# Two expert-layer edits of a hybrid diffusion block: where four query units stand, and how one-hot rows are summed

## The chip, the cores and the metric

The kernel runs on one core of one Trainium2 chip. The metric is the device time of one execution in microseconds. The engines are TensorE (PE; its weight loads are shown as PEld), VectorE (DVE), ScalarE (ACT), GpSimd (POOL) and SyncE (SP, which only starts transfers). ScalarE and GpSimd start transfers too.

## The reference, cut to what matters

Two layers over 256 latent tokens of 1024 values, with 256 context tokens beside them (the context's second layer is needed for its keys and values only). Each layer has a mixer of four branches, and then a product-key expert layer. Only the latter is touched:

```python
def chunk(xc):                                   # 128 tokens
    q = (xc @ wq).reshape(128, 8, 2, 128)
    s1 = einsum('thd,hnd->thn', q[:, :, 0], k1)  # 8 heads, 128 keys
    s2 = einsum('thd,hnd->thn', q[:, :, 1], k2)
    v1, i1 = top_k(s1, 16); v2, i2 = top_k(s2, 16)
    cand = v1[..., :, None] + v2[..., None, :]
    cidx = i1[..., :, None] * 128 + i2[..., None, :]
    top_s, pos = top_k(cand.reshape(128, 8, -1), 16)
    eidx = take_along_axis(cidx.reshape(128, 8, -1), pos, -1)
    g = softmax(top_s, -1)
    h = gelu(einsum('thkd,td->thk', eu[eidx], xc))
    return einsum('thk,thkd->td', g * h, ev[eidx])
```

So each token has 8 x 16 = 128 experts. An expert is one row of 2048 float32 values (1024 of `eu`, 1024 of `ev`).

## The kernel before

**Tiles and passes.** The 256 tokens of a stream are two tiles of 128. Three passes through the expert layer are made: the latent tokens of the first layer (LAT0, `BL0`), the context tokens of the first layer (CTX0, `BC0`), the latent tokens of the second (LAT1, `BL1`). An expert pass goes token by token: GpSimd gathers the 128 rows of a token, one a partition, into one of eight slots of `ring` (L726, 1 MB). TensorE broadcasts the token's own row from `xr` into PSUM (L1215, two halves). VectorE multiplies and sums (L2063, two halves). After four tokens, a group, ScalarE takes the Gelu (L1547), VectorE the weights (L2073), and TensorE sums the `ev` halves (`weigh`, L1197), which sets their four slots free. The rows in `xr` come from DRAM (`xrows`) by small transfers that ScalarE's queue starts (`x_rows`, L1536): those of the first two groups stand in front of a pass's first token, the others behind each Gelu.

**The order of work.** Each engine runs its own program, written out at build time from one `SCRIPT`. A generator `yield`s after each step, and `Weave.run` (L134) then lets `SHARE` tokens of the expert pass follow, the same number on each engine. A step `TILE_READY` makes another 128 tokens available and lets GpSimd ask for up to seven tokens' rows at once (`ask_ahead`, L729). In `ask` (L710), a slot of the first eight is given free only when the query units that read it are multiplied, since `ring` holds the query weights before: token n needs second-tile unit 2n+1 (L723).

**The part in front of an expert pass.** For the two latent passes this is `apart`, written once for each engine (PE L939, ACT L1363, DVE L1955). With no `yield` within it, PE makes 16 query units of the first tile (`unit(0, u)`, eight 128x128 products each, L960) and 16 of the second (`unit(1, u)`). Behind each four of them is one score product (`scores`, L972). ScalarE copies each unit (L1375) and each score group (L1382). VectorE meanwhile searches the first tile's scores (`top16`), joins candidates, decodes positions, and picks the expert numbers (`picked`, L1929). It then hands `ts` to ScalarE for an exponential (`tsub`; `chosen`, L1421), weighs it (`weighted`, L1948) and reports `sel`. PE transposes the expert numbers and weights (L995, L996), ScalarE copies them to `eT` and `gT` (L1425, L1426), and the pass begins. The second tile's searches (`late`, eight steps with 2.4 tokens each, then `sel`) go between the tokens of the first.

**The queues.** Before the change, ScalarE's copies of all 16 second-tile units and of `scores(1, 3)` stand in front of `chosen`. On PE, all of these units, `scores(1, 3)` and the eight turns of `uT` (L993) stand in front of the two transposes. SyncE may load the next tile of `W` when `scores(1, 3)` is done (the `sc_ps` count, L551).

**Picking.** `picked` compares a position with 16 numbers (L1934), multiplies the one-hot rows by the indices (L1936) and sums each row of 16 (L1937). All three are chained by a semaphore, in bf16, with a float32 result. In the first tile of the latent passes it runs over four heads (1024 values a partition), four times. In their second tile and in both context tiles it runs over eight heads (2048), twice each.

Of the kernel before, what the change touches and what calls it, by code (L numbers as in the profile page):

```python
# [7 lines left out]
ALU = mybir.AluOpType  # L8
ACT = mybir.ActivationFunctionType
AX = mybir.AxisListType.X  # L10

D = 1024
P = 128
# [105 lines left out]
TILE_READY = "tile ready"  # L119

LATE = 8

# [90 lines left out]
def build(nc, x, ctx, ccols, cols_c, w_ada, w_rows, w_in, w_gate, w_out, w_q, w_key, b_in, nat_bias, gqa_sink, peer_uv0, peer_uv1,  # L213
          ident_c, wave_c, band_c, iota_c, strip_c, out):
    es = ExitStack()
    with es:
# [36 lines left out]
        ident = sb("ident", [P, P])  # L253
# [65 lines left out]
        isel_a = part(mix, 2 * TILE - 2 * HEADS * TOPK, [2, HEADS * TOPK])  # L319
# [8 lines left out]
        ts = part(small, 1024, [HEADS, TOPK])  # L328
# [13 lines left out]
        def bank(i, a=0, b=512):  # L342
            return PS[:, i * 512 + a:i * 512 + b]
# [398 lines left out]
        def _(pe):  # L742
            T = nc.tensor
# [195 lines left out]
            def apart(b, a):  # L939
# [36 lines left out]
                for u in range(16):  # L976
# [3 lines left out]
                    if u == 6:  # L980
                        pe.wait_ge(a["xn"], a.at("xn", TT))
                        pe.wait_ge(a["xread"], a.at("xread", 1))
                        turned(0, lambda k: scratch[:, 1, k * P:(k + 1) * P]).then_inc(a["xnT"], 1)
                for u in range(16):
                    unit(1, u)
                    if u == 0:
                        scores(0, 3)
                    if u and u % 4 == 0:
                        scores(1, u // 4 - 1)
                scores(1, 3)  # L990
                pe.wait_ge(a["u_ready"], a.at("u_ready", TT))
                pe.wait_ge(a["wo_s"], a.at("wo_s", KD + 32))
                turned(2, lambda k: uT[:, k, P:TOK]).then_inc(a["urow"], 1)  # L993
                pe.wait_ge(a["sel"], a.at("sel", 1))
                T.transpose(bank(6, 0, P), isel_a[:, 0, :], ident[:, :])  # L995
                T.transpose(bank(6, P, 2 * P), ts[:, :, :].rearrange("p h k -> p (h k)"), ident[:, :]).then_inc(a["selT"], 1)  # L996
                yield TILE_READY
                for q in range(LATE):
# [237 lines left out]
        def _(act):  # L1236
# [126 lines left out]
            def apart(b, a):  # L1363
# [30 lines left out]
                for u in range(16):  # L1394
# [5 lines left out]
                    if u == 12:  # L1400
                        rows_out(0)
                for u in range(16):
                    unit(1, u)
                    if u == 0:
                        scores(0, 3)
                    if u and u % 4 == 0:
                        scores(1, u // 4 - 1)
                scores(1, 3)
                chosen(b, a, 0, 6)
                yield TILE_READY  # L1410
                for q in range(LATE):
                    yield "late"
# [150 lines left out]
        def _(dve):  # L1563
# [365 lines left out]
            def picked(tt, h0, nh, e, hot, index):  # L1929
# [6 lines left out]
                ch.link(V.tensor_tensor(one4, one4, iv[:, :, e, :].unsqueeze(2).to_broadcast([P, nh, TOPK, TOPK]), ALU.mult))  # L1936
                ch.link(V.reduce_sum(index[:, e, m0:m1], one, AX))  # L1937

# [267 lines left out]
```

## Time and profile before

| | |
|---|---|
| median of three runs | 3242.15 us (3241.61, 3242.15, 3261.65) |
| the profiled execution | 3264.46 us, span 3262.7 us |
| TensorE busy | 2525.2 us, 77% |
| VectorE busy | 1908.4 us, 58% |
| GpSimd busy | 971.6 us, 30% |
| ScalarE busy | 490.4 us, 15% |
| read from memory | 1011.32 MB |
| mean granted TensorE clock | 0.767 of full |

Busy shares are means over very different stretches: the fronts (units on TensorE), the three selections, and the token loop in which a gather, VectorE and TensorE take turns. Times of a row are counted from the start of the span. A number in square brackets behind a row of a timeline is the time that the engine stood idle before it, and what ended it. TensorE's float32 products are shown as two records each, so 64 records of L960 are four units.

### The profile page before, as it was taken

The numbers are of one execution on the slowest core, as the hardware profiler recorded it, in microseconds if no ns is written. First come the engines' busy times: TensorE is split into PE (matmuls) and PEld (weight loads), VectorE is DVE, ScalarE is ACT, GpSimd is POOL, SyncE is SP. The second block draws the span as 40 slices with busy tenths as digits, with TensorE's granted clock in tenths as the row PEclk, the third lists the DMA queues.
The fourth block names the chain that finished last, engine by engine and source line by source line (L and its number), as shares of the span: only waits on it lengthen the run. The fifth ranks groups of instructions, "written<-read, shape, count | busy, mean of one in ns | idle before, by whom it ended". The sixth has DMA issues, their size and how long they took to land.

```text
span 3262.7 us, 34104 instructions
## 1 busy us (share of the span) xinstructions
PE 2525.2 (77%) x11632; PEld 1304.6 (40%) x11632; DVE 1908.4 (58%) x6024; ACT 490.4 (15%) x1063; POOL 971.6 (30%) x968
## 2 busy tenths in 40 slices
PE   6879986597899978837989987676898557766655
PEld 5768882053355544403544441111788101111111
DVE  3658987746544456785444445555438765555554
ACT  2141120013322210001012220000412000000000
POOL 0730002258222222221672223332000333333332
PEclk7989996587799988756988876656999556566566
DMA  7607737898899988766989999999240889999997
GB/s 307 239 30 291 299 143 286 316 376 299 316 392 370 360 333 354 289 260 264 373 329 411 411 373 389 401 395 367 89 137 11 336 326 402 399 404 372 400 399 299
DMA packets 147887, 1023.54 MB, mean 314 GB/s; under 512 B 18817, under 2 KB 19329, under 8 KB 28033
## 3 DMA queue, kind: packets, MB, share of 16 engines
q0 software_dynamic: 110592, 805.36, 62.1%
q1 hardware_dynamic: 30496, 202.36, 16.0%
q10 hardware_dynamic: 6624, 13.64, 1.1%
q8 instruction: 92, 1.51, 0.2%
q14 instruction: 83, 0.67, 0.1%
HBM read 1011.32 MB, written 9.96 MB: 313 GB/s over the span
## 4 chain that ended last, share of the span: by engine, by line
PE 47%; DMA 20%; DVE 16%; POOL 7%; issue 6%; ACT 3%; ACTq 0%; DVEq 0%; POOLq 0%; SPq 0%
DMA ring<-in_peer_uv,eT 19%; PE PS L1197 12%; PE PS L887 7%; DVE ring L2063 6%; PE PS L1215 6%; POOL ring L726 5%; PE PS L822 3%; PE PS L960 3%; PE PS L908 3%; PE PS L1090 2%; PE PS L892 2%; PE PS L1041 2%; PE PS L1132 1%; DVE ring L1615 1%; POOL mix L609 1%
## 5 line engine op out<-in xcount | busy, mean ns | idle before, releaser
L2063 DVE CUSTOM_DVE_ANT_0 ring<-ring,PS 128x512 f32<-128x512 f32 x1536 | 994.6, 685 | 833.0 <-PE PS L1215 479.7
L726 POOL DMA_INDIRECT ring<-in_peer_uv,eT x768 | 728.5, 949 | 2154.8 <-PE PS L1197 1355.1
L1215 PE MATMUL PS<-xr,onesb 3*128 3x512 bf16 x1536 | 643.6, 485 | 439.7 <-DVE hcol L2063 375.5
L1197 PE MATMUL PS<-ring,zcol 128*32 128x512 f32 x3072 | 592.6, 912 | 104.6 <-DVE zcol L2073 102.3
L1215 PEld LDWEIGHTS PS<-xr,onesb 3*128 3x128 bf16 x1536 | 113.8, 96 | 1053.7 <-DVE hcol L2063 543.0
L1197 PEld LDWEIGHTS PS<-ring,zcol 128*32 128x32 f32 x3072 | 104.1, 143 | 411.9 <-issue 235.9
L887 PE MATMUL PS<-uT,W 128*128 128x256 f32 x1024 | 252.9, 396 | 7.5 <-issue 7.5
L1547 ACT ACTIVATE ge<-hdot 128x4 f32<-128x4 f32 x192 | 39.5, 206 | 1418.3 <-DVE hdot L2068 1379.1
L887 PEld LDWEIGHTS PS<-uT,W 128*128 128x128 f32 x1024 | 195.2, 196 | 67.7 <-issue 41.5
L1615 DVE CUSTOM_DVE_ANT_0 ring<-ring 128x1024 f32<-128x1024 f32 x160 | 205.7, 1326 | 8.2 <-DMA ring<-in_w_rows 3.3
L822 PE MATMUL PS<-uT,W 128*128 128x256 f32 x672 | 170.0, 408 | 18.5 <-ACT uT L1279 18.5
L822 PEld LDWEIGHTS PS<-uT,W 128*128 128x128 f32 x672 | 132.8, 203 | 59.9 <-issue 21.3
L908 PE MATMUL PS<-uT,W 128*128 128x256 f32 x512 | 143.5, 428 | 0.0
L2063 DVE DVE_READ_ACCUMULATOR2_ANT hcol<- 128x1 f32 x1536 | 126.8, 83 | 0.0
L908 PEld LDWEIGHTS PS<-uT,W 128*128 128x128 f32 x512 | 101.2, 208 | 52.7 <-issue 39.6
L960 PE MATMUL PS<-uT,ring 128*128 128x128 f32 x1024 | 120.4, 279 | 0.0
L960 PEld LDWEIGHTS PS<-uT,ring 128*128 128x128 f32 x1024 | 119.1, 196 | 0.0
L1720 DVE TENSOR_TENSOR mix<-sg,PS 128x256 f32<-128x256 f32 x64 | 26.9, 420 | 112.5 <-ACT sg L1339 97.7
L1090 PE MATMUL PS<-mix,W 128*128 128x256 f32 x384 | 87.2, 383 | 2.5 <-DVE mix L1724 1.5
L892 PE MATMUL PS<-mix,W 128*128 128x256 f32 x320 | 79.7, 380 | 0.0
L1090 PEld LDWEIGHTS PS<-mix,W 128*128 128x128 f32 x384 | 71.6, 190 | 19.4 <-issue 7.0
L1547 ACT ACT_TABLE_LOAD x57 | 73.1, 1283 | 37.0 <-DVE mix L1985 27.3
(256 smaller groups left out, 2390.7 us busy)
## 6 DMA issues: line engine op xcount, KB each, us to landing
ring<-in_w_rows SPq DMA_DIRECT2D x40, 1024.0 KB, 8.1
W<-in_w_in SPq DMA_DIRECT2D x30, 1024.0 KB
W<-in_w_gate SPq DMA_DIRECT2D x16, 1408.0 KB
W<-in_w_gate SPq DMA_DIRECT2D x16, 1280.0 KB
ring<-in_w_q SPq DMA_DIRECT2D x16, 1024.0 KB, 12.7
W<-in_w_gate SPq DMA_DIRECT2D x16, 1024.0 KB
W<-in_w_out SPq DMA_DIRECT2D x12, 1024.0 KB
xr<-xrows ACTq DMA_DIRECT2D x768, 6.0 KB
```

Source lines behind the costliest of these rows:

```text
L726: pool.indirect_dma_start(ring[:, slot, :], None, (peer_uv0, peer_uv1)[b.l], bass.IndirectOffsetOnAxis(eT[:, f % 2, t:t + 1], 0)).then_inc ...
L822: last = T.matmul(bank(2 + n % 4, 0, TOK), wk[:, blk * P:(blk + 1) * P], u_[:, k, :], **go)
L887: T.matmul(bank(2 + n % 4, 0, TOK), wg[:, k, g % 2, :], uT[:, k, :], start=(k == 0), stop=(k == KD - 1))
L892: last = T.matmul(bank(2 + n % 4, TOK, 2 * TOK), W[:, slot, TILE + (at - first_kt + k) * P:TILE + (at - first_kt + k + 1) * P], yb[:, at + ...
L908: last = T.matmul(bank(2 + n % 4, 0, TOK), wg[:, k, g % 2, :], uT[:, k, :], start=(k == 0), stop=(k == KD - 1))
L960: last = T.matmul(bank(2 + u % 2, 0, P), ring[:, u // 2, w0:w0 + P], uT[:, k, tt * P:(tt + 1) * P], start=(k == 0), stop=(k == KD - 1))
L1090: last = T.matmul(bank(2 + n % 4, 0, TOK), W[:, slot, k * 2 * P + n % 2 * P:k * 2 * P + (n % 2 + 1) * P], mT[:, k, :], start=(k == 0), sto ...
L1197: last = T.matmul(PS[k * NR:(k + 1) * NR, (6 + h) * 512:(7 + h) * 512], zcol[:, g % 2, k, NR - 1 - at:2 * NR - 1 - at], ring[:, slot, D + ...
L1215: T.matmul(bank(x_bank(q, n) + h), onesb[32 * k:32 * k + 3, :], xr[32 * k:32 * k + 3, g % 2, h * 512:(h + 1) * 512], start=True, stop=True)\
L1547: A(ge[:, g % 2, :], hdot[:, g % 2, :], ACT.Gelu).then_inc(gelu_s, 1)
L1615: last = V.tensor_tensor_reduce(out=w_ if s_ else junk[:, c, :], in0=w_, in1=crow[:, s_, :], scale=1.0, scalar=0.0, op0=ALU.mult, op1=ALU.add,
L2063: V.tensor_tensor_reduce(out=u_half, in0=u_half, in1=bank(x_bank(q, n) + h), scale=1.0, scalar=0.0, op0=ALU.mult, op1=ALU.add, accum_out=h ...
```

## The change

In `apart`, the loop over the second tile's units is cut in two on PE and on ScalarE: units 0 to 11 stay, units 12 to 15 with `scores(1, 2)` and `scores(1, 3)`, and the turns of `uT`, now come after the two transposes on PE and after `chosen` on ScalarE. In `picked` the reduction becomes four additions in place: 8 and 8, 4 and 4, 2 and 2, and the last two into `index`. In the last one the operands have a step of 16 values and the result is float32.

```diff
+AHEAD = 12
 LATE = 8
@@ apart, PE
-                for u in range(16):
+                for u in range(AHEAD):
                     unit(1, u)
                     if u == 0:
                         scores(0, 3)
                     if u and u % 4 == 0:
                         scores(1, u // 4 - 1)
+                pe.wait_ge(a["sel"], a.at("sel", 1))
+                T.transpose(bank(6, 0, P), isel_a[:, 0, :], ident[:, :])
+                T.transpose(bank(6, P, 2 * P), ts[:, :, :].rearrange("p h k -> p (h k)"), ident[:, :]).then_inc(a["selT"], 1)
+                yield TILE_READY
+                for u in range(AHEAD, 16):
+                    unit(1, u)
+                    if u % 4 == 0:
+                        scores(1, u // 4 - 1)
                 scores(1, 3)
                 pe.wait_ge(a["u_ready"], a.at("u_ready", TT))
                 pe.wait_ge(a["wo_s"], a.at("wo_s", KD + 32))
                 turned(2, lambda k: uT[:, k, P:TOK]).then_inc(a["urow"], 1)
-                pe.wait_ge(a["sel"], a.at("sel", 1))
-                T.transpose(bank(6, 0, P), isel_a[:, 0, :], ident[:, :])
-                T.transpose(bank(6, P, 2 * P), ts[:, :, :].rearrange("p h k -> p (h k)"), ident[:, :]).then_inc(a["selT"], 1)
-                yield TILE_READY
@@ apart, ScalarE
-                for u in range(16):
+                for u in range(AHEAD):
                     unit(1, u)
                     if u == 0:
                         scores(0, 3)
                     if u and u % 4 == 0:
                         scores(1, u // 4 - 1)
-                scores(1, 3)
                 chosen(b, a, 0, 6)
                 yield TILE_READY
+                for u in range(AHEAD, 16):
+                    unit(1, u)
+                    if u % 4 == 0:
+                        scores(1, u // 4 - 1)
+                scores(1, 3)
                 for q in range(LATE):
                     yield "late"
@@ picked, VectorE
-                ch.link(V.reduce_sum(index[:, e, m0:m1], one, AX))
+                for half in (8, 4, 2):
+                    ch.link(V.tensor_tensor(one[:, :, 0:half], one[:, :, 0:half], one[:, :, half:2 * half], ALU.add))
+                ch.link(V.tensor_tensor(index[:, e, m0:m1].unsqueeze(2), one[:, :, 0:1], one[:, :, 1:2], ALU.add))
```

## Rows read from the trace of the kernel before

**Rows 1.** The page's chain that ended last, shares of the span by engine.
```profile
PE 47%; DMA 20%; DVE 16%; POOL 7%; issue 6%; ACT 3%; ACTq 0%; DVEq 0%; POOLq 0%; SPq 0%
```

**Rows 2.** Timeline of VectorE, 486 to 545 us: start, us, operation, idle and releaser.
```profile
501.24 0.29 DVE L1940 SCALAR_TENSOR_TENSOR mix<-mix 128x128 f32<-128x128 f32 x1
507.81 0.29 DVE L1950 TENSOR_REDUCE hsum<-small 128x8 f32<-128x128 f32 x1 [6.28 <-ACT small L1423]
...
516.08 0.69 DVE L2063 CUSTOM_DVE_ANT_0 ring<-ring,PS 128x512 f32<-128x512 f32 x1 [4.68 <-DMA ring<-in_peer_uv,eT]
...
518.67 0.69 DVE L2063 CUSTOM_DVE_ANT_0 ring<-ring,PS 128x512 f32<-128x512 f32 x1 [1.29 <-DMA ring<-in_peer_uv,eT]
...
522.76 0.69 DVE L2063 CUSTOM_DVE_ANT_0 ring<-ring,PS 128x512 f32<-128x512 f32 x1
...
524.26 0.69 DVE L2063 CUSTOM_DVE_ANT_0 ring<-ring,PS 128x512 f32<-128x512 f32 x1 [0.20 <-PE PS L1215]
...
532.40 0.69 DVE L2063 CUSTOM_DVE_ANT_0 ring<-ring,PS 128x512 f32<-128x512 f32 x1 [0.75 <-DMA ring<-in_peer_uv,eT]
```

**Rows 3.** Timeline of ScalarE and its queue (ACTq), 484 to 545 us.
```profile
495.92 0.28 ACT L1375 ACTIVATE mix<-PS 128x128 f32<-128x128 f32 x1 [1.51 <-PE PS L960]
...
505.49 0.60 ACT L1382 ACTIVATE scratch<-PS 128x512 f32<-128x512 f32 x1 [1.25 <-PE PS L972]
...
509.19 0.49 ACTq L1536 DMA_DIRECT2D xr<-xrows  x1
```

**Rows 4.** Timeline of GpSimd, 484 to 545 us: the first gather.
```profile
509.92 1.11 POOL L726 DMA_INDIRECT ring<-in_peer_uv,eT  x1 [316.67 <-ACT gT L1426]
```

**Rows 5.** Timeline of TensorE, 484 to 545 us: the transpose and the first broadcast.
```profile
508.71 0.33 PE L995 MATMUL PS<-ident,mix 128*128 128x128 f32 x1 [2.39 <-DVE small L1952]
...
511.89 1.01 PE L1215 MATMUL PS<-xr,onesb 3*128 3x512 bf16 x2 [2.74 <-DMA xr<-xrows]
```

**Rows 6.** Timeline of VectorE in the second latent layer, 2510 to 2580 us.
```profile
2531.55 0.29 DVE L1950 TENSOR_REDUCE hsum<-small 128x8 f32<-128x128 f32 x1 [6.27 <-ACT small L1423]
...
2539.50 0.69 DVE L2063 CUSTOM_DVE_ANT_0 ring<-ring,PS 128x512 f32<-128x512 f32 x1 [4.36 <-DMA ring<-in_peer_uv,eT]
...
2542.36 0.69 DVE L2063 CUSTOM_DVE_ANT_0 ring<-ring,PS 128x512 f32<-128x512 f32 x1 [1.55 <-DMA ring<-in_peer_uv,eT]
```

**Rows 7.** The chain in order of time, 500 to 700 us: start, us, what.
```profile
618.23 2.30 DVE mix L1937
```

**Rows 8.** Timeline of TensorE, 405 to 450 us: the end of work and its return.
```profile
420.71 3.74 PE L793 MATMUL PS<-ident,cols 128*128 128x128 f32 x32
...
436.34 1.94 PE L936 MATMUL PS<-ident,uT 128*128 128x128 f32 x8 [3.14 <-ACT uT L1279]
```

**Rows 9.** Windows: PE, PEld, DVE, ACT, POOL busy, then clock, DMA share, GB/s.
```profile
427.00:428.00 1.00, 0.00 (x0) 0.00 (x0) 0.96 (x3) 0.00 (x0) 0.00 (x0) 0.67 0.99 418
...
440.00:441.00 1.00, 1.00 (x6) 1.00 (x6) 0.97 (x2) 0.00 (x0) 0.00 (x0) 0.51 1.04 434
...
516.00:526.00 10.00, 4.51 (x8) 0.80 (x8) 8.02 (x33) 0.20 (x1) 2.81 (x3) 0.50 1.01 424
```

**Rows 10.** The page's DMA queue of the gathers: packets, MB, share of 16 engines.
```profile
q0 software_dynamic: 110592, 805.36, 62.1%
```

**Rows 11.** Timeline of SyncE's queue, 425 to 700 us.
```profile
505.48 185.46 SPq L466 DMA_DIRECT2D W<-in_w_in  x3
```

**Rows 12.** Groups of VectorE instructions by line and form: count, busy us, mean ns.
```profile
L1937 DVE TENSOR_REDUCE mix<-mix 128x128 f32<-128x2048 bf16 x8 | 18.3, 2286 | 0.3
...
L1936 DVE TENSOR_TENSOR mix<-mix,small 128x2048 bf16<-128x2048 bf16 x8 | 9.8, 1224 | 0.3
L1937 DVE TENSOR_REDUCE mix<-mix 128x64 f32<-128x1024 bf16 x8 | 9.8, 1220 | 0.3
...
L1936 DVE TENSOR_TENSOR mix<-mix,small 128x1024 bf16<-128x1024 bf16 x8 | 5.5, 692 | 0.3
...
L1927 DVE TENSOR_TENSOR small<-mix 128x128 bf16<-128x128 f32 x6 | 1.7, 284 | 0.0
```

## The prediction

> **What bounds the kernel now.** I read the page's chain first. It is made of TensorE for 47%, DMA for 20%, VectorE for 16% and GpSimd for 7% [rows 1], so no engine alone is the bound, and a stretch has to be read before an edit in it can be priced. I then read three stretches that the diff touches, engine by engine in the order of time.
>
> The first is the end of the first selection of the first latent layer (about 496 to 533 us). VectorE ends the first tile's expert numbers with L1940 at 501.53 us. It then stands still for 6.28 us until L1950 at 507.81, released by ScalarE [rows 2]. ScalarE does not make the exponential (L1423) when its input is there, but when its queue comes to it: behind the copies of the second tile's last units and the last score copy (505.49 + 0.60 us) [rows 3]. That is the wait which the change goes at: `chosen` moves up behind unit 11's copy (495.92 + 0.28 us).
>
> What follows matters more. The first expert row is dotted at 516.08 us, after 4.68 us of waiting for its gather, the second at 518.67 after 1.29 us for its own, the seventh at 532.40 after 0.75 us [rows 2]. Two things must be there for a dot: the gather, which GpSimd first issues at 509.92 [rows 4], and the broadcast of the token's row by TensorE (L1215), which needs small transfers into xr that ScalarE's queue issues at 509.19 [rows 3], for a first broadcast at 511.89 [rows 5]. So today the gather is the later by about 3.4 us (516.08 less 0.75 of dot after broadcast, less 511.89). The second latent layer has the same picture: L1950 waits 6.27 us, the first dots wait 4.36 and 1.55 us for gathers [rows 6].
>
> The third view is the chain inside the later selections: the one-hot reduction is on it with its whole length, 2.30 us [rows 7]. One row stands for eight: the chain holds each reduction of 128x2048 so.
>
> **The moved units.** Nothing is added or removed: four units, two score groups and the eight turns of uT run on TensorE after the two transposes instead of before, and their copies run on ScalarE after `chosen`.
>
> Before `chosen`: ScalarE ends unit 11's copy at 496.20. From the end of the last score copy (506.09) to L1950 it is 1.72 us, so the exponential would be seen at 497.9, before VectorE is done. The wait of 6.28 us goes: L1950 starts at 501.53 plus what the additions add (0.1, below), with the usual step of 0.03 after a link, 501.65; that is 6.15 earlier. The transposes (L995 at 508.71 [rows 5]) come to 502.55, the first gather to 503.8. Gathers then land from about 510 (6.15 us from issue to dot today).
>
> Behind it: TensorE starts unit 12 at about 502.9. Today from unit 11's copy (495.92) to the last score copy (505.49) it is 9.57 us [rows 3]. To this comes the clock. TensorE stands idle from 496.0 to 502.55, 6.5 us that are new. After its work ended at 420.71 + 3.74 us the granted clock fell between 427 and 428 (0.67 in it), and when it took up work again at 436.34 it was 0.50, its low level of 1.2 GHz, almost to 441 (0.51 in 440 to 441), for 4.6 us [rows 8, 9]. So it will be low when unit 12 starts and stay low for some 4.6 us after 502.55; half of the 4.3 us of it that lie on the units is lost, 2.2 us. Bounds: nothing if it doesn't fall, 9.6 us if it stays low to the end of the four units. I take 2.2, the nearest row.
>
> The Trainium skill, "TensorE: Matmul & The Clock Gate", section "Why this matters for your kernels", speaks against this edit: it says not to leave TensorE idle between bursts of matmuls, since its clock falls. By that rule, the 2.2 us stand; without it they would be zero. The rows at 427 and 440 us agree.
>
> The last score copy starts at 502.9 + 9.6 + 2.2 = 514.7. The requests for xr stand behind it in ScalarE's queue (token 0 comes after all of `apart`'s units in the woven order), where today they stand behind L1425. So they go out at 514.7 instead of 509.19. The first broadcast comes 2.70 us later, 517.4, and the first dot 0.75 later, 518.15. It was 516.08: **the start of the experts is 2.1 us later, though the gathers start 6 us earlier.** What is late next is no longer the gather but the xr rows.
>
> The second dot comes 1.50 us behind the first, as between 522.76 and 524.26 where no transfer is waited for [rows 2]: 519.65, 1.0 later than today. From there VectorE has the late searches of the second tile between the tokens, and these set the pace. The seventh token's 0.75 us for its gather goes. GpSimd may ask for token 6 when unit 13 and for token 7 when unit 15 is multiplied (its wait on `wo`), at the latest near 514. A gather is 805.36 MB / 768 = 1.05 MB, and at the 424 GB/s of 516 to 526 us it takes 2.5 us [rows 9, 10], so with SyncE's next 1 MB tile of W, which today goes out at 505.48 upon the last scores [rows 11] and will go out in the midst of them, for another 2.5, token 6 lands by about 529, before its 532. So +1.0 - 0.75 = +0.25 us in this layer. The second one: L1950 at 2531.55 - 6.15 = 2525.4; from it 16.5 us to the first dot as above, 2541.9 against 2539.50; the second dot 2543.4 against 2542.36, +1.0. No later gather wait is known there, so +1.0 stands. Sum of the move: **+1.25 us**, bounds by the clock: if it doesn't fall, the second dot comes 1.2 us earlier than today in both layers, with the 0.75 some -3.2; low to the end, 7.4 more in each, some +16.
>
> **The additions.** 16 reductions go: eight of 128x1024 (1220 ns) and eight of 128x2048 (2286 ns) [rows 12]. Each becomes three halvings in bf16 and a last addition of strided bf16 into float32. No row shows a two-operand addition of bf16 over rows of 8, 4 or 2. The nearest is L1936, all bf16: 692 ns for 1024 and 1224 for 2048 elements, that is 160 ns and 0.52 ns an element. By it the halvings take: of 2048, 0.69 + 0.42 + 0.29, and the last as L1927, 128 elements with float32 on one side, 0.28; in all 1.68, with three more links of 0.03 us 1.78. Saved are 0.5 us each. Of 1024: 0.42 + 0.29 + 0.22 + 0.22 + 0.1 = 1.25, which is 0.03 more than now. The other bound is one element at a time (the reductions' own 1.04 ns an element, and 1.22 us for 1024): 1.22 + 0.69 + 0.42 + 0.28 + 0.1 = 2.71, 0.42 more; and 1.72, 0.5 more. I take the first, since L1936 has the same type, operands and unit steps, only longer runs.
>
> The small ones stand in front of the two `sel` (0.1 us each, counted above). The eight large ones are on the chain: 8 x 0.5 = **-4.0 us**. At the slow bound it is +3.4 and, with the small ones, +7.4. If other waits take the gain, it is 0.
>
> **Sum.** +1.25 - 4.0 = -2.75 us. The profiled execution took 3264.46 us (span 3262.7), so the sum gives 3261.7 for it. The three timed runs are 3241.61, 3242.15 and 3261.65: the profiled one stands with the slowest, 22 us above the median. On the median the sum gives 3239.4, some 0.1% less, which the timing will not tell from nothing (1%, about 32 us, is what it can tell).
>
> **Rivals.**
> - *The wait goes for good.* If the xr rows did not hang behind the units, the dots would follow the gathers: 6.15 us earlier in two layers, 12.3, with the additions -16: 3226. For it: the 6.28 us are real and the gathers do go out earlier. Against: ScalarE's order. Chance 0.10.
> - *Slower: the low clock.* Where TensorE stays at 0.50 for more than about 7.4 us after `sel` (2 x 1.4 us lost beside the 2.2), both layers lose more than the additions bring. At the worst, low through all four units, it is +16 - 4 = +12: 3254. For it: 0.50 in 516 to 526 us, when TensorE works with gaps [rows 9]; against: the units are dense work, in which the clock rose by 441. Chance 0.17.
> - *The additions don't double their rate.* +1.25 + 7.4 = +8.5: 3250. A short row of two elements may cost as much as a long one. Chance 0.10.
> - *Nothing of the additions is kept*, because the tokens that follow wait for gathers or for TensorE anyway: +1.5: 3243.5. Rows 7 speak against it, the 20% of DMA in the chain for it. Chance 0.13.
>
> **How the numbers follow.** My own case has 0.45, with 3235 to 3243. All the cases lie within 1% of before. The 0.05 left is for a shift in how gathers and W tiles meet, which no row can price. So: faster by over 1% 0.03, within 1% 0.94, slower 0.03. The range goes from the first rival, 3226, to a median that falls where the slowest run before fell, 3262.
>
> **What would show it.** In the new profile: no wait before L1950; a TensorE gap of 6.5 us in front of L995 and a clock of 0.50 behind it; the last four units behind L995; the first dot not before 517.5 us and VectorE idle some 12 us before it, released by the broadcast and not by a gather; 1.8 us for the four additions on 2048 elements. If the first dot is at 512, my reading of ScalarE's queue is wrong; if the halvings of 1024 take 1.2 us, the rate is.

## The result, and the profile after

| | before | after |
|---|---|---|
| median of 20 runs each | 3250.82 us (3238.01 to 3261.65) | 3261.46 us (3251.36 to 3273.39) |
| the profiled execution | 3264.46 us, span 3262.7 | 3254.91 us, span 3252.7 |

The ratio is 1.0041, with a 95% interval from 1.0030 to 1.0052: the change costs 13.3 us (9.8 to 16.9). I had forecast 2.75 us less. (The 3242.15 us that the forecast was added to came from three runs; twenty give 3250.82, so only the ratio can be held against it. The quotient of the two medians is 1.0033, or 10.6 us; it lies within the interval too.) The time is within 1%, but the sign is wrong, and the error of 16 us is far more than the measurement's own.

The profiled execution of after is shorter than the one shown of before, though its kernel is the slower one. Single executions spread by 20 us, so no difference of 13 us can be read from two spans. I compare stretches instead, counted from an event that both kernels have: ScalarE's copy of unit 11.

The chain that ended last, by engine, in the page of after. Against [rows 1], TensorE has 4 points less and VectorE 4 more:

```profile
PE 43%; DMA 20%; DVE 20%; POOL 7%; issue 5%; ACT 3%; ACTq 0%; DVEq 0%; POOLq 0%; SPq 0%
```

Timeline of VectorE in after, first latent layer (start, us, operation, idle before it and its releaser):

```profile
499.48 0.29 DVE L1962 TENSOR_REDUCE hsum<-small 128x8 f32<-128x128 f32 x1
...
523.69 0.69 DVE L2075 CUSTOM_DVE_ANT_0 ring<-ring,PS 128x512 f32<-128x512 f32 x1 [20.61 <-PE PS L1221]
...
525.19 0.69 DVE L2075 CUSTOM_DVE_ANT_0 ring<-ring,PS 128x512 f32<-128x512 f32 x1 [0.20 <-PE PS L1221]
```

L1962 is L1950 of before. It has no wait in front of it, where it had 6.28 us in [rows 2]. But the first dot (L2075, L2063 of before) comes after 20.61 us of idleness, and its releaser is the broadcast (L1221, once L1215), no longer a gather. Timeline of ScalarE and its queue in after:

```profile
493.14 0.28 ACT L1381 ACTIVATE mix<-PS 128x128 f32<-128x128 f32 x1 [1.51 <-PE PS L962]
...
494.73 0.31 ACT L1433 ACTIVATE small<-small 128x128 f32<-128x128 f32 x1
...
513.59 0.60 ACT L1388 ACTIVATE scratch<-PS 128x512 f32<-128x512 f32 x1 [1.25 <-PE PS L974]
513.60 2.83 ACTq L1546 DMA_DIRECT2D xr<-xrows  x8
```

From unit 11's copy to the first dot it is now 523.69 - 493.14 = 30.55 us. In before it was 516.08 - 495.92 = 20.16 [rows 2, 3]. The requests for xr go out at 513.60, behind the last score copy. Timeline of GpSimd in after, the first gather and the eighth:

```profile
501.84 1.11 POOL L728 DMA_INDIRECT ring<-in_peer_uv,eT  x1 [311.30 <-ACT gT L1436]
...
512.29 0.94 POOL L728 DMA_INDIRECT ring<-in_peer_uv,eT  x1 [1.89 <-PE PS L962]
```

All eight gathers of 1 MB are asked for before the eight small transfers of xr (6 KB each: three rows of 1024 bf16). In before the first of them went out at 509.19 [rows 3], ahead of the first gather at 509.92 [rows 4]. The other seven followed up to 511.89, and the gathers' bytes began to flow only about 511.5 (the DMA engines moved 22 GB/s from 509.92 to 511.40). Timeline of TensorE in after, first and second latent layer:

```profile
500.39 0.48 PE L993 MATMUL PS<-ident,mix 128*128 128x128 f32 x1 [7.28 <-DVE small L1964]
...
505.99 5.75 PE L962 MATMUL PS<-uT,ring 128*128 128x128 f32 x48
512.40 1.16 PE L974 MATMUL PS<-W,mix 128*128 128x128 f32 x8 [0.66 <-ACT mix L1381]
513.39 1.04 PE L938 MATMUL PS<-ident,uT 128*128 128x128 f32 x8
522.93 1.00 PE L1221 MATMUL PS<-xr,onesb 3*128 3x512 bf16 x2 [8.51 <-DMA xr<-xrows]
...
2510.53 0.47 PE L993 MATMUL PS<-ident,mix 128*128 128x128 f32 x1 [7.19 <-DVE small L1964]
...
2530.66 1.01 PE L1221 MATMUL PS<-xr,onesb 3*128 3x512 bf16 x2 [6.09 <-issue]
```

From the request to the first broadcast it is 522.93 - 513.60 = 9.33 us. In [rows 3, 5] it was 511.89 - 509.19 = 2.70. (The broadcast waits for the first four of the eight.) This is the number that the loss hangs on; I call it the step from request to broadcast. In the second layer the request is at 2523.80, so the step is 6.86 us there, against 2.47 in before.

### The profile page after: what moved, and what is told of

It is laid out like the page before. It is cut to its first block, busy times and chain, and to the rows that moved or that the text cites. A ratio compares the mean times of both kernels' runs of the same rounds, so it can differ in the third digit from the quotient of the medians.

```text
span 3252.7 us, 34152 instructions
## 1 busy us (share of the span) xinstructions
PE 2515.7 (77%) x11632; PEld 1305.6 (40%) x11632; DVE 1902.6 (58%) x6072; ACT 490.2 (15%) x1063; POOL 970.6 (30%) x968
## 3 DMA queue, kind: packets, MB, share of 16 engines
q8 instruction: 92, 1.51, 0.2%
## 4 chain that ended last, share of the span: by engine, by line
PE 43%; DMA 20%; DVE 20%; POOL 7%; issue 5%; ACT 3%; ACTq 0%; DVEq 0%; POOLq 0%; SPq 0%
DMA ring<-in_peer_uv,eT 19%; PE PS L1203 11%; PE PS L889 7%; DVE ring L2075 7%; PE PS L1221 5%; POOL ring L728 5%; PE PS L824 3%; PE PS L1096 3%; PE PS L894 2%; PE PS L962 2%; PE PS L1047 2%; PE PS L910 2%; POOL mix L611 1%; DVE ring L1625 1%; PE PS L930 1%
## 5 line engine op out<-in xcount | busy, mean ns | idle before, releaser
L2075 DVE CUSTOM_DVE_ANT_0 ring<-ring,PS 128x512 f32<-128x512 f32 x1536 | 994.2, 685 | 845.9 <-PE PS L1221 486.0
L1221 PE MATMUL PS<-xr,onesb 3*128 3x512 bf16 x1536 | 646.2, 486 | 433.2 <-DVE hcol L2075 367.4
L1203 PE MATMUL PS<-ring,zcol 128*32 128x512 f32 x3072 | 584.3, 901 | 106.3 <-DVE zcol L2085 104.1
L1221 PEld LDWEIGHTS PS<-xr,onesb 3*128 3x128 bf16 x1536 | 114.8, 96 | 1052.3 <-DVE hcol L2075 565.3
L889 PE MATMUL PS<-uT,W 128*128 128x256 f32 x1024 | 251.1, 394 | 7.5 <-issue 7.5
L824 PE MATMUL PS<-uT,W 128*128 128x256 f32 x672 | 167.9, 405 | 18.3 <-ACT uT L1285 16.3
L910 PE MATMUL PS<-uT,W 128*128 128x256 f32 x512 | 140.0, 420 | 0.0
L2075 DVE DVE_READ_ACCUMULATOR2_ANT hcol<- 128x1 f32 x1536 | 126.7, 82 | 0.0
```

The source lines that it names most:

```text
L824: last = T.matmul(bank(2 + n % 4, 0, TOK), wk[:, blk * P:(blk + 1) * P], u_[:, k, :], **go)
L889: T.matmul(bank(2 + n % 4, 0, TOK), wg[:, k, g % 2, :], uT[:, k, :], start=(k == 0), stop=(k == KD - 1))
L910: last = T.matmul(bank(2 + n % 4, 0, TOK), wg[:, k, g % 2, :], uT[:, k, :], start=(k == 0), stop=(k == KD - 1))
L1203: last = T.matmul(PS[k * NR:(k + 1) * NR, (6 + h) * 512:(7 + h) * 512], zcol[:, g % 2, k, NR - 1 - at:2 * NR - 1 - at], ring[:, slot, D + ...
L1221: T.matmul(bank(x_bank(q, n) + h), onesb[32 * k:32 * k + 3, :], xr[32 * k:32 * k + 3, g % 2, h * 512:(h + 1) * 512], start=True, stop=True)\
L2075: V.tensor_tensor_reduce(out=u_half, in0=u_half, in1=bank(x_bank(q, n) + h), scale=1.0, scalar=0.0, op0=ALU.mult, op1=ALU.add, accum_out=h ...
```

## The experiments

All eleven experiments are in one table. A dot is counted from unit 11's copy; "12th" is the first dot of the twelfth token, when the start has passed and the tokens follow at their own pace. "Sum" is what the two 12th dots gained or lost against before. "Timed" is the ratio less 1, times 3247 us.

| kernel | ratio (95%) | first dot, layers 1 and 2 | 12th dot, layers 1 and 2 | sum | timed |
|---|---|---|---|---|---|
| before | 1 | 20.16, 19.84 | 52.52, 51.84 | 0 | 0 |
| after | 1.0041 (1.0030 to 1.0052) | 30.55, 28.04 | 60.70, 58.60 | +14.9 | +13.3 |
| e1_move_only | 1.0040 (1.0024 to 1.0055) | 29.72, 27.37 | 60.12, 57.73 | +13.5 | +13.0 |
| e2_adds_only | 1.0001 (0.9989 to 1.0013) | 20.59, 19.57 | 53.35, 52.28 | +1.3 | +0.3 |
| e3_xr_early | 0.9998 (0.9983 to 1.0012) | 21.77, 21.76 | 51.97, 51.98 | -0.4 | -0.6 |
| e9_gathers_wait | 1.0063 (1.0042 to 1.0083) | 33.07, 29.22 | 65.48, 61.25 | +22.4 | +20.5 |
| e4_ahead14 | 1.0012 (0.9998 to 1.0026) | 23.46, 21.95 | 53.60, 52.68 | +1.9 | +3.9 |
| e5_filler | 1.0034 (1.0023 to 1.0046) | 30.75, 28.03 | 61.43, 58.72 | +15.8 | +11.0 |
| e6_xr_filler | 0.9993 (0.9981 to 1.0006) | 22.43, 21.34 | 53.01, 51.84 | +0.5 | -2.3 |
| e8_exp_only | 0.9980 (0.9967 to 0.9992) | 17.96, 17.15 | 49.75, 49.47 | -5.1 | -6.5 |
| e7_split14 | 0.9973 (0.9957 to 0.9989) | 13.86, 18.55 | 48.69, 48.98 | -6.7 | -8.8 |
| e11_split15 | 0.9970 (0.9954 to 0.9985) | 14.12, 13.41 | 49.55, 45.97 | -8.8 | -9.7 |
| e12_split15_adds8 | 0.9979 (0.9966 to 0.9993) | 14.04, 13.51 | 48.94, 45.74 | -9.7 | -6.8 |

Over thirteen kernels the two last columns stay within 5 us of each other; the intervals of the ratios are 4 to 7 us either way. So, to that accuracy, the time is made and lost at the start of the two latent expert passes, and what happens there can be read from one profile.

**Each half of the change alone.**

```diff
 e1_move_only: after, with the reduction of before
-                for half in (8, 4, 2): ... four additions
+                ch.link(V.reduce_sum(index[:, e, m0:m1], one, AX))
 e2_adds_only: before, with the four additions of after
```

> The move alone (units 12 to 15 behind the transposes), the reduction of before kept. Theory A (the requests for the xr rows leave ScalarE behind the moved copies, when gathers fill the DMA engines, and wait among them): the first broadcast comes some 9 us after its request in the first latent layer and some 7 us in the second, where before it was 2.7 and 2.5; the second dot comes 9 and 7 us later after unit 11 than before; the time is 0.4 to 0.5% above before (+13 to +16 us). Rival B (the additions made the changed kernel slower, the move is worth little): within 0.1% of before.

> The additions alone, order of the units as before. Theory A: they save 0.3 us on each of the eight 128x2048 sums and lose 0.14 us on each of the eight 128x1024 ones; the small ones stand in front of a wait of 6.28 us for the exponential and are hidden there, so the time is 2 to 3 us (0.07%) below before, and the wait before the weighting shrinks to about 5.7 us. Rival B (the additions are what cost): 0.3 to 0.4% above before.

The move alone gives 1.0040, the whole change 1.0041: all of the loss that the timing can see belongs to the move. Its steps from request to broadcast are 9.23 and 6.80 us, as expected, and its second dots come 8.5 and 6.2 us later than in before, a little less than the 9 and 7 expected. The additions alone give 1.0001 and no part of the loss. After's groups of VectorE instructions by line and form (count, busy us, mean ns, idle) say why they bring so little:

```profile
L1948 DVE TENSOR_TENSOR mix<-mix 128x512 bf16<-128x512 bf16 x16 | 6.8, 426 | 0.5
L1948 DVE TENSOR_TENSOR mix<-mix 128x1024 bf16<-128x1024 bf16 x8 | 5.5, 692 | 0.3
L1948 DVE TENSOR_TENSOR mix<-mix 128x256 bf16<-128x256 bf16 x16 | 5.5, 341 | 0.5
L1949 DVE TENSOR_TENSOR mix<-mix 128x128 f32<-128x128 bf16 x8 | 3.1, 388 | 0.3
L1948 DVE TENSOR_TENSOR mix<-mix 128x128 bf16<-128x128 bf16 x8 | 2.2, 276 | 0.3
L1949 DVE TENSOR_TENSOR mix<-mix 128x64 f32<-128x64 bf16 x8 | 2.2, 274 | 0.3
```

The halvings into rows of 8 and 4 run at the rate that I took (692 and 426 ns). The 341 ns of 256 elements are a mean of two cases, eight with rows of 4 and eight with rows of 2. And the last addition, one element of each row at a step of 16 values, takes 388 ns for 128 elements, where I had 284. The timeline of VectorE in after, a selection over four heads and one over eight, gives each set as a whole:

```profile
490.88 1.06 DVE L1948 TENSOR_TENSOR mix<-mix 128x512 bf16<-128x512 bf16 x3
491.97 0.27 DVE L1949 TENSOR_TENSOR mix<-mix 128x64 f32<-128x64 bf16 x1
...
611.50 1.58 DVE L1948 TENSOR_TENSOR mix<-mix 128x1024 bf16<-128x1024 bf16 x3
613.11 0.39 DVE L1949 TENSOR_TENSOR mix<-mix 128x128 f32<-128x128 bf16 x1
```

The large set takes 2.00 us against 2.30 [rows 7], so 0.3 is saved and not 0.5; the small one 1.36 against 1.22 [rows 12], so 0.14 is lost and not 0.03. By these durations the large sets save 8 x 0.3 = 2.4 us. The small ones cost 4 x 0.14 before each `sel`, 1.1 us in all, where nothing hides them, as in after: some -1.3 us. In e2_adds_only they are hidden in the wait for the exponential, which is 6.02 us there (I had expected 5.7), so it should have gained 2.4. An interval of 4 us either way shows neither.

**The xr rows in front of the gathers.** The edit takes the requests for xr out of the pass and puts them in front of `chosen`, behind unit 11's copy; nothing else of after changes.

```diff
+                rows_in(0)          # the four small transfers of group 0
+                rows_in(1)          # and of group 1
                 chosen(b, a, 0, 6)
                 yield TILE_READY
 ...
-                        if n == 0:
+                        if n == 0 and not OF[f].apart:
```

> The changed kernel, with the requests for the xr rows of the first two groups put in front of the exponential, so before any gather. Theory A: they have landed long before they are wanted; the first broadcast follows the eight turns of uT without a wait, the first dot comes about 22 us after unit 11's copy instead of 30.5 (first latent layer), and the time falls by 13 to 15 us against the changed kernel, to within 0.1% of before. Rival C (the low TensorE clock or the gathers set the start of the dots): the first dot stays 28 us or more behind unit 11's copy, released by something else, and the time stays 0.3% or more above before.

The queue of ScalarE in this kernel, and after it the timeline of its TensorE:

```profile
493.08 2.70 ACTq L1398 DMA_DIRECT2D xr<-xrows  x8
```

```profile
500.34 0.47 PE L993 MATMUL PS<-ident,mix 128*128 128x128 f32 x1 [7.31 <-DVE small L1976]
...
513.31 1.04 PE L938 MATMUL PS<-ident,uT 128*128 128x128 f32 x8
514.28 0.60 PE L1221 MATMUL PS<-xr,onesb 3*128 3x512 bf16 x2
```

The broadcast now follows the turns of uT with no wait. The first dot is 8.8 and 6.3 us earlier than in after, and the ratio goes from 1.0041 to 0.9998. The low clock, the moved units and the additions are all still there. So the loss hangs on the time between the request for xr and its landing, and the low clock alone does not make it. Of the gathers' earlier start nothing is kept either, because the broadcast now stands behind TensorE's own work: 21.77 us to the first dot, where before had 20.16.

**The gathers out of the way.** The opposite test: after, with the first gather held until the xr rows have landed. This gives away some 18 us of gathering and isn't meant to be fast.

```diff
+                if b.apart and n == 0:
+                    pool.wait_ge(xr_land[1], 16 * (q * NG // 2 + 1) * GRP)
```

> The changed kernel, with GpSimd's first gather of the two latent passes held back until the xr rows of both groups have landed. Theory A (the xr rows are late because the gathers are in the DMA engines before them): the first broadcast now comes 2.7 us behind the first xr request, as before the change, instead of 9.3 and 6.9 us; the first dot then waits for its gather, about 10.5 us behind the request, so the time stays within 0.2% of the changed kernel. Rival E (the requests themselves are slow, by ScalarE's queue or by where they stand): the first broadcast stays 7 us or more behind the request.

The queue of ScalarE in this kernel, first and second layer, and then its TensorE:

```profile
514.65 2.70 ACTq L1548 DMA_DIRECT2D xr<-xrows  x8
...
2536.80 2.51 ACTq L1548 DMA_DIRECT2D xr<-xrows  x8
```

```profile
519.90 1.01 PE L1223 MATMUL PS<-xr,onesb 3*128 3x512 bf16 x2 [4.42 <-DMA xr<-xrows]
...
2539.43 0.59 PE L1223 MATMUL PS<-xr,onesb 3*128 3x512 bf16 x2 [1.85 <-issue]
```

In the second layer, with almost nothing else in the DMA engines (14 GB/s), the step is 2539.43 - 2536.80 = 2.63 us, where before had 2.47. With the gathers it was 6.86. So they cost 4.2 us. In the first layer it is still 5.25, not the 2.7 that I had expected. SyncE asks for the next 1 MB of W at the very same time there (514.64; the second layer has no such request). That is 2.6 us more, and with the gathers in flight the two layers differ by the same: 9.33 - 6.86 = 2.5. So 9.33 is about 2.7 + 4.2 for the gathers + 2.5 for the tile of W. No run holds that tile back by itself, but e8_exp_only (below) agrees: it asks for xr 0.7 us ahead of the first gather in both layers, and in the first also for the tile, 1.1 us before xr (505.64). Its step is 4.58 us in the first layer and 2.52 in the second. The first layer:

```profile
506.75 0.49 ACTq L1543 DMA_DIRECT2D xr<-xrows  x1
...
511.33 1.01 PE L1215 MATMUL PS<-xr,onesb 3*128 3x512 bf16 x2 [4.63 <-DMA xr<-xrows]
```

The 2.5 us are what I had worked out for 1 MB in the prediction, spent in a place where I hadn't looked. The first dots of e9_gathers_wait come 12.9 and 10.4 us behind the request (10.5 expected), and its ratio is 0.22 points above after's, at the edge of the 0.2% that I had expected.

**Fewer gathers in front.** If small transfers stood in line behind all bytes asked for before, four gathers in front would delay them less than eight.

```diff
-AHEAD = 12
+AHEAD = 14
```

> The changed kernel with 14 units in front of the transposes and 2 behind, nothing else. Theory A (the start is set by how many gathers are asked for before the xr rows): the xr rows are requested some 4 to 5 us behind the first gather instead of 12, with three or four gathers before them instead of eight; the first broadcast comes 3 to 7 us behind the request, the first dot about 21 us behind unit 11's copy (30.5 and 28 in the changed kernel, 20 before), and the time is 10 to 14 us below the changed kernel, within 0.1% of before. Rival G (any unit behind the transposes costs the same, since the requests wait for all gathers in any case): the first dot stays at 26 us or more and the time at 0.25% above before or more.

The queue of ScalarE in this kernel, and its TensorE:

```profile
508.22 2.79 ACTq L1546 DMA_DIRECT2D xr<-xrows  x8
```

```profile
517.62 1.01 PE L1221 MATMUL PS<-xr,onesb 3*128 3x512 bf16 x2 [8.57 <-DMA xr<-xrows]
```

Only four gathers have been asked for before the request here (the fourth at 507.75), yet the step takes 9.40 us, and in the second layer 6.85, with five. These are the 9.33 and 6.86 of after. I had expected 3 to 7 us, and it did not shrink.

The number of gathers asked for is not what is in flight, though: some have landed by then. After's windows in its second layer, from the first gather to the request and from there to the broadcast (the last number is GB/s), give the bytes:

```profile
2511.97:2523.80 11.83, 9.95 (x80) 9.57 (x80) 1.19 (x7) 1.66 (x6) 7.41 (x8) 0.94 0.85 316
2523.80:2530.66 6.86, 0.77 (x8) 0.56 (x6) 0.00 (x0) 1.82 (x2) 0.08 (x1) 0.74 1.01 424
```

Of 8.4 MB asked for, 11.83 us x 316 GB/s = 3.7 MB had moved at the request, so 4.7 were outstanding; in e4_ahead14's second layer it is 5.2 - 1.4 (5.80 us at 244 GB/s) = 3.8. If xr stood behind all of it, the step would be some 2 us shorter there, and 4.7 MB would have to move before the broadcast of after. The step is the same, and only 6.86 x 424 = 2.9 MB moved. So the small transfers did not stand behind all bytes asked for before. Whether the delay would shrink with much less in flight is not tested.

The kernel is faster than after (1.0012) because the request itself goes out 7.2 us earlier after unit 11's copy (13.30 against 20.46), and the first dot is 7.1 us earlier with it.

The Trainium skill, "DMA: Bandwidth & Descriptors", section "Queues, rings and completion order", says that each DMA engine takes turns between the queues that have work, a whole packet at a time. That fits small transfers that overtake part of the gathers' bytes. Why the turns cost 4.2 us beside the gathers and 2.5 beside the tile of W is not shown by any run here.

**Does the low clock cost anything?** First a filler of 28 transposes in front of the wait for `sel`, in after; then 58 of them on top of e3_xr_early.

```diff
+                for _ in range(28):        # 58 in e6_xr_filler
+                    T.transpose(bank(7, 0, P), uT[:, 0, 0:P], ident[:, :])
                 pe.wait_ge(a["sel"], a.at("sel", 1))
```

> The changed kernel, with 28 more transposes on TensorE (into an unused bank, results not used) in the 6.5 us in which it waits for sel, so that its clock doesn't fall. Theory A: the granted clock stays at 1.00, the four units take 7.2 instead of 9.4 us, the xr rows are requested 2 us earlier but still wait among the gathers; the time is 2 to 6 us below the changed kernel, still 0.2% or more above before. Rival C (the clock is what cost): 10 us or more below the changed kernel, within 0.1% of before.

> The kernel with the early xr requests (e3_xr_early), and 58 transposes more on TensorE (results not used) in the 6.5 us in which it waits for sel, so that it works nearly to the end of that wait. Now nothing but TensorE's own work sets the first broadcast. Theory A (the clock is one smaller term): the granted clock stays at 1.00 through the four units, unit 12 to the last scores take 9.6 instead of 11.9 us, and the first dot comes 2.2 us earlier after unit 11 than in e3_xr_early (19.6 instead of 21.8); the time falls by 4 us. Rival D (the clock doesn't follow TensorE's work here, the units stay slow): no change of either.

Timeline of TensorE with 28 transposes:

```profile
495.53 3.22 PE L993 MATMUL PS<-ident,uT 128*128 128x128 f32 x28
502.99 0.48 PE L995 MATMUL PS<-ident,mix 128*128 128x128 f32 x1 [4.23 <-DVE small L1966]
503.25 0.42 PE L996 MATMUL PS<-ident,small 128*128 128x128 f32 x1
503.47 3.62 PE L962 MATMUL PS<-uT,ring 128*128 128x128 f32 x16
```

The transposes took only 3.22 us, and 4.23 us of idleness were left. The granted clock was 1.00 during the filler and 0.50 when work came back (502.99 to 507.00), and the first transpose and unit 12 (16 records) ran as slowly as in after (0.48 and 3.62 us). So this run can't say what a full clock would bring. Its time, 1.0034, can't be told from after's. Timeline of TensorE with 58 transposes:

```profile
493.83 6.50 PE L993 MATMUL PS<-ident,uT 128*128 128x128 f32 x58
...
501.58 1.95 PE L962 MATMUL PS<-uT,ring 128*128 128x128 f32 x16
...
512.88 1.16 PE L974 MATMUL PS<-W,mix 128*128 128x128 f32 x8 [3.11 <-ACT mix L1383]
```

Here the clock held (unit 12 in 1.95 us instead of 3.62; granted 1.00 from 494 to 513). TensorE gained 2.4 us with it up to unit 13, and then lost it again: it waited 3.11 us for ScalarE's copy. Timeline of ScalarE in the same kernel:

```profile
511.03 0.28 ACT L1383 ACTIVATE mix<-PS 128x128 f32<-128x128 f32 x1 [4.51 <-PE PS L962]
512.55 0.28 ACT L1383 ACTIVATE mix<-PS 128x128 f32<-128x128 f32 x1 [1.25 <-remote]
```

The ratio, 0.9993, can't be told from e3_xr_early's 0.9998, and the first dot is no earlier (22.43 and 21.34 against 21.77 and 21.76). The gain of 4 us expected of the full clock is not seen. Those copies come every 1.79 us elsewhere (0.28 + 1.51), and they came so in e9_gathers_wait too, where no gather was in flight. With gathers in flight some come late in after, e1, e3, e5, e6 and the second layer of e4; the worst, in e1_move_only, had 4.81 us of idleness before it instead of 1.51. What holds them up, which the trace calls "remote" or puts down to products long done, no run here shows. So the price of the clock in time is not measured: another wait lies right under it.

**Taking the wait away without moving anything.** The same 6.28 us can be had with one line: the exponential alone goes behind unit 11's copy, in before.

```diff
                     if u and u % 4 == 0:
                         scores(1, u // 4 - 1)
+                    if u == 11:
+                        exponential(0)
                 scores(1, 3)
-                chosen(b, a, 0, 6)
+                chosen(b, a, 0, 6, False)   # without its exponential
```

> The kernel of before, with one edit: the exponential stands behind unit 11's copy on ScalarE instead of behind the last scores. All units stay in front of the transposes. Theory A: the wait of 6.28 us before the weighting goes, sel is there at about 502.5 us of the old count, the transposes follow TensorE's own turns of uT at once, 2.3 us earlier than before; xr rows and gathers are asked for 2.3 us earlier, and the time falls by 3 to 5 us (0.1 to 0.15%). Rival F (something else takes its place, as the small first transfers): no change.

Timeline of VectorE in this kernel:

```profile
501.72 0.29 DVE L1957 TENSOR_REDUCE hsum<-small 128x8 f32<-128x128 f32 x1
...
514.04 0.69 DVE L2070 CUSTOM_DVE_ANT_0 ring<-ring,PS 128x512 f32<-128x512 f32 x1 [8.73 <-DMA ring<-in_peer_uv,eT]
```

The wait is gone, TensorE never stands idle for `sel`, and xr is still asked for before the gathers. The ratio is 0.9980, 6.5 us less (2.6 to 10.7) where I had expected 3 to 5, and the first dot comes 2.2 and 2.7 us earlier. The other 4 us of the 6.28 are not won by this edit: they are TensorE's work on the units, which the transposes still stand behind.

**All of it in a better order.** From after: reduction instead of additions, the exponential behind unit 11, the xr requests behind units 7 and 9, and only the last two units (then the last one) behind the transposes.

```diff
-AHEAD = 12
+AHEAD = 14                         # 15 in e11_split15
 ...
+                    if u in (7, 9):
+                        rows_in((u - 7) // 2)
+                    if u == 11:
+                        exponential(0)
-                chosen(b, a, 0, 6)
+                chosen(b, a, 0, 6, False)
```

> A version meant to keep what the move was after: reduction as before; exponential behind unit 11's copy; the xr requests of both groups behind units 7 and 9, so before any gather; 14 units in front of the transposes and 2 behind. Theory A: TensorE waits about 2 us for sel and keeps its full clock; gathers are asked for 6 us earlier, the first broadcast follows some 6 us behind the transposes, and the first dot comes about 14 us behind unit 11's copy (20.2 before), the second at 18; 10 to 12 us in all, 0.3% below before. Rival F (the later tokens wait for their gathers instead, so that the start is worth nothing): within 0.1% of before.

> The version e7_split14 with 15 units in front and 1 behind. TensorE then waits only some 0.3 us for sel, and only one unit's copy and one score copy on ScalarE fall into the time of the gathers. Theory A: the clock stays at 1.00 in both layers, the first dots are set by their gathers (14 us behind unit 11's copy in both layers, where e7_split14 had 13.9 and 18.6), and the time is 1 to 3 us below e7_split14, about 0.3% below before. Rival F (the later dots wait for gathers anyway): no difference from e7_split14.

> The version e11_split15 with the additions where they were seen to be shorter than the reduction (128x2048, eight times) and the reduction where they were longer (128x1024). Theory: 8 x 0.3 = 2.4 us below e11_split15, if all of it is on the chain; if the tokens behind them wait for their gathers, nothing.

e12_split15_adds8 is e11_split15 with the four additions for eight heads only, where they are shorter than the reduction. Timeline of VectorE in e11_split15:

```profile
506.79 0.69 DVE L2092 CUSTOM_DVE_ANT_0 ring<-ring,PS 128x512 f32<-128x512 f32 x1 [4.88 <-DMA ring<-in_peer_uv,eT]
...
513.02 0.69 DVE L2092 CUSTOM_DVE_ANT_0 ring<-ring,PS 128x512 f32<-128x512 f32 x1 [4.92 <-DMA ring<-in_peer_uv,eT]
```

The first dot is now 6 us earlier than in before and again released by its gather, so the transfers bound the start. Not all of it is kept: the second dot waits 4.92 us for its own gather, and at the twelfth token 3.0 us are left in the first layer, 5.9 in the second. Two things in the second layer of e7_split14 did not come as expected. The first dot came only after 18.55 us, behind 9.32 us of idleness that "remote" ended; whether that is the same open cause as above is not known. And the clock did not hold: TensorE stood idle for 2.10 us and was then granted 0.50 from 2505 to 2508. In the first layer of the same kernel it kept 1.00 after 2.09 us of idleness, and so it did in both layers of e11_split15 after 0.33. e7_split14 and e11_split15 are the fastest kernels of this case, 0.9973 and 0.9970 (8.8 and 9.7 us less than before, where I had expected 10 to 12 of e7_split14); their intervals overlap. With the additions for eight heads it is 0.9979, again overlapping: the 2.4 us that their durations promise did not show in the time, and whether they exist behind the tokens' other waits stays open.

## Why the prediction was wrong

The step that failed is the time from the request for xr to the first broadcast: I took 2.70 us, and it was 9.33 and 6.86. By the prediction's own steps:

- **The wait in front of L1950 goes: right.** L1962 has none, and the first gather goes out 8.70 us after unit 11's copy (501.84 - 493.14) instead of 14.00 [rows 3, 4].
- **TensorE stands idle, and its clock falls: right, and about in size.** I said 6.5 us of idleness; it was 7.28. Windows of after (busy time of PE, PEld, DVE, ACT and POOL, granted clock, DMA share, GB/s):

```profile
495.00:500.00 5.00, 0.00 (x0) 0.00 (x0) 4.52 (x12) 0.04 (x1) 0.00 (x0) 0.62 0.00 0
500.00:501.00 1.00, 0.61 (x3) 0.62 (x4) 0.93 (x6) 0.00 (x0) 0.00 (x0) 0.50 0.02 8
...
506.00:507.00 1.00, 1.00 (x9) 1.00 (x9) 0.00 (x0) 0.60 (x1) 0.70 (x2) 0.78 1.11 418
507.00:508.00 1.00, 1.00 (x12) 1.00 (x10) 0.00 (x0) 0.00 (x0) 0.92 (x1) 1.00 0.88 369
```

  It was low for about 6 us after work came back at 500.39, where [rows 8, 9] had given 4.6. From unit 12's first product to the next group TensorE took 5.12 us in after (500.87 to 505.99) and 2.68 in e6_xr_filler (501.58 to 504.26), so 2.4 us went; I had 2.2. The second layer lost 1.2 (3.86 us for the same, 2511.01 to 2514.87), where I had 2.2 too. The Trainium skill, "TensorE: Matmul & The Clock Gate", says in "Why this matters for your kernels" that TensorE should not be left idle between bursts of matmuls, since its clock falls. The trace agrees (0.62 in 495 to 500, 0.50 when work came back). But this is not what made the kernel slower.
- **The xr requests stand behind the last score copy: right.** I had them 18.8 us after unit 11's copy (514.7 - 495.92). They went out after 20.46 and 20.42. Of the 1.7 us more, 0.6 are in front of L1962 (6.34 after the copy against 5.73), with the additions' extra 0.11 us four times in it, and 0.3 are in the 0.66 in front of L974 (about 0.37 where nothing disturbs). 0.2 are the clock, and the other 0.6 or so are not assigned.
- **"The first broadcast comes 2.70 us later": this step failed.** It took 9.33 and 6.86 us. I carried the 2.70 of [rows 3, 5] over to a place with other work in the DMA engines. In before, the first of the eight went out 0.7 us ahead of the first gather, and the four that the broadcast waits for had gone before the gathers' bytes began to flow. Moved behind the units they went out when eight gathers had been asked for and some 4.6 MB of them were outstanding, and in the first layer with a tile of W. I had even counted these transfers ("a gather ... takes 2.5 us, so with SyncE's next 1 MB tile of W ... another 2.5"), but as something that delays token 6, not the 6 KB that everything waits for. This is 6.6 + 4.2 = 10.8 us of the 14.1 by which the two second dots came later than I had forecast (9.3 + 6.8 against 2.0). The other 3.3 are the requests' 1.7 and 1.6 us. e3_xr_early takes it away and the loss with it; in e9_gathers_wait's second layer, without gathers and without the tile of W, the step is 2.63 us again.
- **The second dot 1.0 us later, +0.25 and +1.0 in the two layers: wrong by the step above.** It came 9.3 and 6.8 us later; the pace behind it was as I said. The seventh token's wait for its gather is gone, and so the first layer has 8.2 at the twelfth token, 1.1 less than at the second.
- **The additions -4.0 us: the term was mis-sized**, -2.4 by the durations, with +1.1 instead of some +0.2 for the small ones. The durations that were wrong are the last addition's (388 ns for 284) and those of the shortest halvings (276 for 220). None of it can be seen in the time of e2_adds_only (1.0001) or of e12_split15_adds8.

Put together from the runs: +14.9 at the two twelfth tokens, the small additions being in it, and -2.4 for the large ones by their durations, +12.5 us; measured +13.3 (9.8 to 16.9).

Of the rivals, "Slower: the low clock" gave +12, nearly the right number, by luck and for a wrong reason: the clock was low for 6 us and not through all four units. Had I looked only at the total, I would have taken the clock for the cause. "The wait goes for good" assumed that xr did not hang behind the units. That is e3_xr_early, and even it brings nothing, since the broadcast is then behind the units themselves.

## What to carry to other kernels

A latency that you read for a small transfer holds for the traffic that surrounded it; when an edit moves the request, look at what the other queues have in flight at the new place, and price it again. Keep small transfers that something waits for ahead of the large ones that can wait, above all ahead of gathers that an earlier step releases. And where an engine waits for one short instruction in a full queue, move that instruction (e8_exp_only) before moving the queue around it.

## What the runs showed of the hardware

- From the first request of eight 6 KB transfers to the use of the first four it took 2.5 to 2.7 us with nearly free DMA engines (before, e8, e9), 5.25 beside one 1 MB load, 6.8 to 6.9 with gathers in flight and 9.2 to 9.5 with both (after, e1, e4, e5). It was no less with 3.8 MB of gathers outstanding (e4) than with 4.7 (after).
- TensorE was granted 0.50 after 7.28 us of idleness in after and after 4.23 in e5_filler; 58 transposes in such a gap kept it at 1.00 (e6_xr_filler). In e4_ahead14 it kept 1.00 after 3.29 and 2.94 us, and in e7_split14 it kept it after 2.09 us in one layer and lost it after 2.10 in the other.
- ScalarE's copies, every 1.79 us when no gather was in flight, came up to 3.3 us late when gathers were (4.81 of idleness instead of 1.51), some with "remote" as releaser. The cause is open.
- An addition of bf16 pairs at a step of 16 values into float32 took 388 ns for 128 elements and 274 for 64; a contiguous one of 128, of other types (float32 into bf16), took 284 [rows 12], so the step's own share is not shown.
